# Ranking the product-key scores where the matmul left them: one copy per set taken out of the expert search

## The reference, cut to what matters

```python
qh = (xblk @ w_q).reshape(PEER_BLOCK, PEER_HEADS, 2, PEER_DQ // 2)
s = jnp.einsum('nhpd,pkd->nhpk', qh, sub_keys).astype(jnp.float32)   # 8 heads x 2 halves x 128 keys
sv, si = lax.top_k(s, K)                                             # K = 16 of each 128
cand = (sv[:, :, 0, :, None] + sv[:, :, 1, None, :]).reshape(...)    # 16 x 16 sums per head
fv, fpos = lax.top_k(cand, K)                                        # 16 of 256
...
act = jax.nn.gelu(jnp.einsum('nd,nhkd->nhk', xblk, u_tab[eidx]), approximate=False)
return jnp.einsum('nhk,nhkd->nd', (gate * act).astype(xblk.dtype), v_tab[eidx])
```

## Time and profile before

| what | us |
|---|---|
| median of three runs | 3994.39 |
| lowest of the three | 3993.17 |
| highest of the three | 13917.62 |
| the profiled execution, its own time | 3981.78 |
| its span, first to last instruction | 3980.0 |

### The profile page before, as it was taken

How to read it: one execution, slowest core, us unless ns; L and a number is a source line. 1 busy time by engine, 2 the same in 40 slices (tenths; PEclk the granted TensorE clock), 3 DMA queues, 4 the chain that set the end, 5 groups by cost and what they waited for, 6 DMA issues and landing times.

```text
span 3980.0 us, 46682 instructions
## 1 busy us (share of the span) xinstructions
PE 3103.8 (78%) x16448; PEld 1371.4 (34%) x16448; DVE 2403.3 (60%) x5612; ACT 1570.8 (39%) x4397; POOL 1278.6 (32%) x1202
## 2 busy tenths in 40 slices
PE   6699999596787778678777867877787788767777
PEld 1466565454223224123323423342332333214111
DVE  1355544237569558756955774596569447848744
ACT  0233332232543453364345335434533453333333
POOL 0000000022444344444433443443344334444432
PEclk9899999597788689689968977896788789778689
DMA  9773536764999999999999999999999999999998
GB/s 380 285 245 123 195 124 52 294 222 166 412 402 397 415 411 399 404 410 402 400 409 380 400 400 373 393 403 417 371 397 399 403 371 395 404 380 400 417 414 364
DMA packets 238950, 1395.82 MB, mean 351 GB/s; under 512 B 41812, under 2 KB 68308, under 8 KB 92020
## 3 DMA queue, kind: packets, MB, share of 16 engines
q0 software_dynamic: 168480, 1198.61, 75.1%
q1 hardware_dynamic: 65224, 173.65, 13.4%
q10 hardware_dynamic: 5012, 20.58, 1.3%
HBM read 1365.02 MB, written 94.27 MB: 367 GB/s over the span
## 4 chain that ended last, share of the span: by engine, by line
DMA 27%; PE 23%; DVE 20%; ACT 8%; issue 2%; POOL 1%; ACTq 0%; SPq 0%; POOLq 0%; DVEq 0%
DMA mem<-in_experts,mem 24%; PE psum L1421 10%; DVE mem L1744 10%; PE psum L1299 3%; DVE mem L1589 3%; DVE mem L1588 3%; DMA mem<-qkv_rows 2%; PE psum L1274 2%; PE psum L1327 2%; ACT L1528 1%; DVE mem L1591 1%; ACT mem L1532 1%; ACT mem L1529 1%; PE psum L1260 1%; PE psum L1228 1%
## 5 line engine op out<-in xcount | busy, mean ns | idle before, releaser
L1421 PE MATMUL psum<-mem 64*64 64x512 f32 x8192 | 1392.2, 772 | 657.6 <-ACT mem L1532 656.0
L1744 DVE CUSTOM_DVE_ANT_0 mem<-mem 128x1024 f32<-128x1024 f32 x1088 | 1324.6, 1221 | 771.3 <-DMA mem<-in_experts,mem 761.6
L1219 POOL DMA_INDIRECT mem<-in_experts,mem x1088 | 1213.8, 1116 | 1772.0 <-PE psum L1421 1606.7
L1528 ACT ACTIVATE mem<-mem 128x1 f32<-128x1 f32 x1088 | 219.2, 201 | 1501.3 <-DVE mem L1744 1500.0
L1421 PEld LDWEIGHTS psum<-mem 64*64 64x64 f32 x8192 | 269.3, 159 | 1410.7 <-ACT mem L1532 1214.5
L1532 ACT ACTIVATE mem<-mem 128x64 f32<-128x64 f32 x1088 | 379.1, 348 | 35.6
L628 PE MATMUL psum<-mem 128*128 128x512 f32 (+3 forms) x864 | 339.0, 544 | 11.0 <-ACT mem L588 9.8
L1529 ACT ACTIVATE mem<-mem 128x1 f32<-128x1 f32 x1088 | 320.4, 294 | 35.3
L1327 PEld LDWEIGHTS psum<-mem 128*128 128x128 f32 x2304 | 286.9, 203 | 100.7 <-issue 93.6
L1327 PE MATMUL psum<-mem 128*128 128x128 f32 (+1 forms) x2304 | 312.2, 291 | 3.3 <-ACT mem L1479 3.0
L628 PEld LDWEIGHTS psum<-mem 128*128 128x128 f32 (+1 forms) x864 | 147.4, 188 | 176.2 <-issue 162.4
(11 more groups left out here) (266 smaller groups left out, 2747.8 us busy)
## 6 DMA issues: line engine op xcount, KB each, us to landing
out_k_s<-in_cache_k SPq DMA_DIRECT2D x8, 4080.0 KB, 17.6
out_v_s<-in_cache_v SPq DMA_DIRECT2D x8, 4080.0 KB, 29.6
mem<-in_w_ada SPq DMA_DIRECT2D x12, 2048.0 KB, 15.2
mem<-in_experts,mem POOLq DMA_INDIRECT x1088, 10.4
mem<-in_vals POOLq DMA_DIRECT2D x16, 1024.0 KB, 7.8
mem<-in_keys_t POOLq DMA_DIRECT2D x14, 1024.0 KB, 6.0
mem<-in_x SPq DMA_DIRECT2D x16, 512.0 KB, 14.8
mem<-in_w_in ACTq DMA_DIRECT2D x2, 3072.0 KB, 25.4
```

The lines of the kernel that those rows point to most:

```text
L1219: pool.indirect_dma_start(out=ring[:, g % N_SLOTS].rearrange("p a n -> p (a n)"), out_offset=None, in_=ins["experts"][:, :], in_offset=bas ...
L1421: mm = nc.tensor.matmul(psum[(LOW, HIGH)[half], tok.start // HALF_P], diag[tok, g % 4], ring[tok, g % N_SLOTS, 1, cols], start=c == 0, sto ...
L1528: chain.link(a.activation(weight[:, c:c + 1], dots[:, c:c + 1], ACT.Gelu))
L1744: v.tensor_tensor_reduce(row, row, h2[i % 2], 1.0, 0.0, ALU.mult, ALU.add, dots[:, c:c + 1]).then_inc(sig["dots"], 1)
```

## The change

The scores are no longer copied. The first MAX8, the first FIND_INDEX8 and the MATCH_REPLACE8 of a set read PSUM bank 6 or 7 directly; MATCH_REPLACE8 writes `rest` in SBUF as before and now carries the count of `found`, so that TensorE gets the bank back after it. The second MAX8 and FIND_INDEX8 read `rest`. The buffer's place in SBUF is kept free, so that no other address moves. The ranking of the 16 x 16 sums is unchanged.

```diff
-    found = work.take(2, NKEY)
+    work.take(2, NKEY)
...
                     dve.wait_ge(sig["s_ps"], 2 * HEADS * n + j + 1)
-                    v.tensor_copy(found[R, j % 2], psum[R, 6 + j % 2, 0:NKEY]).then_inc(sig["found"], 1)
+                    scores, left = psum[R, 6 + j % 2, 0:NKEY], rest[R, j % 2]
+                    chain.link(v.max(top_v[R, hh, half, 0:8], scores))
+                    chain.step(v.max_index(top_i[R, hh, half, 0:8], top_v[R, hh, half, 0:8], scores))
+                    v.match_replace(left, top_v[R, hh, half, 0:8], scores, -3.0e38).then_inc(sig["found"], 1)
                     dve.wait_ge(sig["found"], 2 * HEADS * n + j + 1)
-                    best(top_v[R, hh, half], top_i[R, hh, half], found[R, j % 2], rest[R, j % 2])
+                    chain.link(v.max(top_v[R, hh, half, 8:16], left))
+                    chain.step(v.max_index(top_i[R, hh, half, 8:16], top_v[R, hh, half, 8:16], left))
```

## The result

The changed kernel takes 3952.63 us in the median of four runs, against 3999.53 for the kernel before: a ratio of 0.9886, 95% interval 0.9867 to 0.9905. One of the four runs of the kernel before took 13917.62 us; the ratio leaves it out, and the other three have a median of 3994.39. So it is about 1% faster, or a little less.

The account below looks back on a forecast made before the run. VectorE was taken to bound picks 80 to 104 of seven windows, gathers elsewhere. Savings of 27.3 + 1.0 + 1.1 = 29.4 us from the timed median 3994.4 gave 3965.0 us, range 3944 to 3996.

Parts of the forecast that it names:

- What bounds the kernel: Picks 80 to 104 of the seven windows ranking tiles 1 to 7: VectorE late, busy 61.66 of 63.78 us; elsewhere gathers.
- The copy: VectorE's copy of scores from PSUM before each set's first MAX8: removing it saves 0.32 us per set.
- The reads: First MAX8, FIND_INDEX8 and MATCH_REPLACE8 from PSUM: 13 ns more each, leaving 0.28 us saved per set, range 0.23 to 0.35.
- pair of equal two-source operations: Profile rows of VectorE operations with two sources, same shape: 692 ns with PSUM, 689 without, suggesting no extra read price.
- equal fixed parts: Time beside the per-column cost: 153 ns for a copy from PSUM, 164 for MAX8 from SBUF, so PSUM no dearer.
- the two tensor-scalars: Tensor-scalar rows of 128 x 64: 285 ns from PSUM, 255 from SBUF; 30 ns taken as upper bound per read.
- The sum: Tiles 1 to 7: 14 of 16 sets at 0.28 us, 3.9 us per window, 27.3 us over seven windows.
- What is late next: Picks 80 to 104 after the change: 60.7 us against the gathers' floor of 59.9; VectorE still later unless gaining over 0.35 per set.
- The bank: PSUM bank returned to TensorE 0.66 us later, after MATCH_REPLACE8: 7.2 us of cover, no cost; rival that TensorE waits, 2%.
- the renamed wait: VectorE waits for `found` before the second MAX8 instead of the chain's count, both ended by MATCH_REPLACE8: no cost.
- tiles 0 and 8: Searches in the opening window and of the 64-token last tile: 1.1 and 1.0 us gained, most copies covered.
- the likeliest case: The forecast itself, given 60%: 3965 us, own range 3953 to 3976.

Follow-up runs that it names:

- dead copy: Changed kernel with VectorE copying each set's scores unused before ranking them from PSUM: one copy per set, ratio to before 0.9993; two copies, 1.0112.
- The second measurement: The changed kernel timed again with nothing edited, against the kernel before: median 3966.88 us, ratio 0.9905 (0.9873 to 0.9936).

## Why the prediction was right

*What bounds the kernel.* Right. VectorE had no idle time before L1744 in the dense part, and taking time from it there shortened that part by 3.4 to 3.5 us in each of the seven windows; each dead copy lengthened it by 3.6.

*The copy.* 0.32 us a set was the size: 63.78 - 60.32 = 3.46 us over 11 sets is 0.315, and the 12 to 14 ns of the reads bring it to 0.33.

*The reads.* I took 13 ns a read between bounds of -11 and +30; it is 12 to 14 for all three, so a third of it. The pair of equal two-source operations and the equal fixed parts were the better guide, and the two tensor-scalars a poor one. The estimate of 65 ns more a read, worked out from the table of the Trainium skill (*VectorE: DVE Perf Modes*, "The TRN2 errata"), does not show in any run here.

*The sum.* 0.28 us over 14 sets made 3.9 a window, 27.3 together; the profiles give 875.80 - 848.11 = 27.7. Two sizes were off against each other: a set gains 0.315, and fewer than 14 sets' worth stays. Sixteen would give 5.0 a window, 4.0 stayed, and of the 1.0 that went into waits for gathers most went at picks 72 to 80, as I had said; I had counted two of the four sets there as lost, and nearly three were (6.1 of 8.8 us). That the sums agree within 0.4 us is therefore in part luck.

*What is late next.* I called VectorE the later one after the change, narrowly, and put the crossing at 0.35 us a set. The run without MATCH_REPLACE8 shows the gathers right behind: the changed kernel already stands at their pace. So the crossing lies about where the change has come to, 0.315 us a set, and not at 0.35. In that run picks 72 to 120 took 1.5 to 2 us more than the floor of 119.7, for a reason that is not shown.

*The bank, the renamed wait, tiles 0 and 8.* The first two cost nothing, as said; the 2.1 us that I gave tiles 0 and 8 are too small to see.

*The total.* 29.4 us were forecast, to 3965.0. The 3952.63 that came lies inside the stated range, but just under the 3953 at which the likeliest case's own range ended, and 42 us below the 3994.39 of before. The second measurement has 29 us by the medians (3995.52 to 3966.88) and 38 by the ratio. The pair of kernels with the copy put back by tiles, timed beside each other, has 28.4, which is what the search explains (27.7), so the forecast's size is borne out and the larger gain of the first measurement is not. Nothing shows where more could come from: in all twelve profiles picks 0 to 72 took 1444 to 1471 us, in the kernels that copy in tiles 1 to 7 (1447 to 1470) as in those that do not (1444 to 1471). Whether the excess is more than scatter stays open. The 12.6 us by which the timed runs of before stood above the profiled execution did not carry over: the changed kernel's profiled execution took 3956.0 us, 3 more than its median.

## What to carry to other kernels

Look at the time per unit of work stretch by stretch, and compare it with the pace where nothing but the transfers limits: the difference is the most that any saving in that stretch can bring, and an operation saved elsewhere brought nothing that could be measured (here 32 of 144 copies). When a matmul's result is read by three operations such as these, on 128 columns of floats, and then never again, read it in PSUM; a copy would have to buy something else, such as an earlier return of the bank, and here that had cover. And judge a change of under one per cent by the stretch that it touches, where two profiles of the same kernel agree within 0.03 us, rather than by the total, which differs by 40 us between the two.

## What was new about the hardware

VectorE's MAX8 over 128 x 128 floats takes 295 ns from PSUM and 295 from SBUF, FIND_INDEX8 291 and 285, MATCH_REPLACE8 281 and 276. Two opposite edits, the copy on ScalarE and the copy as dead work, give 12 and 14 ns a set for the three.

The gathers reach 418 or 419 GB/s in the search too, in the run in which VectorE waits for them, next to 420 in the window that does nothing else. In picks 80 to 104 the DMA share read 0.98 to 1.01 before, at 389 to 409 GB/s, and 1.01 after, at 413 to 419: it says little of whether the gathers were held up, and GB/s says more.
